# A fused transformer block on one core: 46 instead of 36 expert units beside the selection matrix, in matmuls of 512 columns, five blocks of u in front of the picks, and a parked unit first

## The chip, the cores and the metric

The kernel runs on one core of a Trainium2 chip. The metric is the device time of one execution in microseconds (us), less is better. Engines are named as in the profile: PE does matmuls, ACT is ScalarE, DVE is VectorE, POOL is GpSimd, SP only issues transfers here.

## The reference

Two transformer blocks on 256 tokens of 1024 features in fp32. The change touches only the last layer of the second block, a "PEER" layer: for every token it selects 8 x 16 of 16384 experts, and each expert is a row of u and a row of v.

```python
s = jnp.einsum('thpd,hpnd->thpn', q, sub_keys)
sv, si = lax.top_k(s, k)
...
experts = jnp.take_along_axis(cand_idx, top_i, axis=-1)
g = jax.nn.softmax(top_v, axis=-1)
u_e = u[experts]
v_e = v[experts]
a = jax.nn.gelu(jnp.einsum('td,thkd->thk', xb, u_e).astype(jnp.float32), approximate=False)
return jnp.einsum('thk,thkd->td', (g * a).astype(xb.dtype), v_e)
```

## The kernel before

The kernel gathers nothing. It computes the Gelu of every expert with every token, multiplies by a matrix G (experts by tokens) that holds the softmax weight where the expert was picked and zero elsewhere, and multiplies the product with all of v. Experts are handled in 64 units of 256.

**fp32 as pairs.** Each fp32 operand is split in a rounded part "hi" and a remainder "lo", and a product is three: hi by hi, hi by lo, lo by hi. Weights come in blocks of 512 KB through a ring of five slots: SP issues the load when PE has released the slot, ACT writes hi (L1051), DVE (L1437) or POOL (L2085) writes lo. Beside G all remainders are POOL's. A unit of u is two such blocks (b = 0, 1), a unit of v is two as well.

**Two forms of a block of u.** `feature_panel` (L654, L659) takes the tokens' hi and lo in two matmuls of 256 columns that add up in one PSUM bank per unit. `unit_panel` (L681, L686) streams tokens' hi and lo as one matmul of 512 columns; the products with hi and with lo then lie in two halves of a bank, a unit needs two banks, and somebody must add the halves. Before, only the main part uses the second form: DVE copies one half and adds the other (L2035, L2036).

**Stages.** "Select" finds the picks: DVE works through top-16 lists while PE computes scores and the first 11 units of u. Then the stage "beside G": after two blocks of u, PE transposes the picks (L1008); from there on 64 steps of G (four tokens each) lie between the blocks of u of 36 units. A step of G is: DVE compares (L1984, L1987), ACT scales (L1388), DVE scales the rest (L1994), PE does four matmuls (L1017) in two halves of a bank each, ACT copies one part of the result (L1375), DVE adds the other (L2001), which frees the bank. ACT and DVE do the result of step q - 2 in step q (`HOT_BUFS`). The finished u units go through Gelu (`early_out`, L1345) and are parked in DRAM.

**Main part.** `UNIT_ORDER` mixes the 17 units of u that are left with the 47 parked ones. PE does a unit's u when its turn comes and, `V_LAG` = 2 turns later, its v (L716, L721: 24 matmuls of 512 columns onto four accumulator banks). In between DVE multiplies by G (L2042), ACT rounds (L1406), DVE takes the remainder (L1738).

**The order** is written out by generators that every engine walks: `expert_matrix_order` yields u blocks, the picks and G steps, and a constant (`GELU_LATER`) says how many items later ACT does the Gelu. Each engine takes its own list in order and waits on semaphores. Banks come from `take(..., among=...)`: the first idle one of a group, in the order in which they became idle.

Of the kernel before, what the change touches and what calls it, by code (L numbers as in the profile page):

```python
# [30 lines left out]
T = 256  # L31
# [22 lines left out]
for _name, _n in (("norm_mix_g", 8), ("q_norm_g", 3), ("kv_norm_g", 2), ("b_gate", 16), ("norm_ffn_g", 8),  # L54
# [17 lines left out]
HID_BUFS = 3  # L72
# [4 lines left out]
EARLY_BESIDE_G = 36  # L77
# [20 lines left out]
    early=(22528, 23040, 23552, 52288),  # L98
# [186 lines left out]
def build(nc, a, out, parked_x, parked_g2, parked_units):  # L285
    from contextlib import ExitStack
    ctx = ExitStack()
    with ctx:
# [71 lines left out]
        def psum(*key):  # L360
            return banks[use_of[key][0]]
# [66 lines left out]
        early_stored = [sem(f"early{i}_stored") for i in range(4)]  # L428
# [155 lines left out]
        def tensor_program(e):  # L584
# [451 lines left out]
        def scalar_program(e):  # L1036
# [385 lines left out]
        def vector_program(e):  # L1422
# [580 lines left out]
            for what, n, b in expert_matrix_order():  # L2003
                if what == "u":
                    lo_until(("uT", n), b, 1)
                elif what == "picks":
                    for t in range(NT):
# [8 lines left out]
                else:  # L2016
# [4 lines left out]
            for q in range(N_G - HOT_BUFS, N_G):  # L2021
                G_sum(q)
# [217 lines left out]
        def sync_program(e):  # L2240
# [56 lines left out]
            sp.wait_ge(g2_parked, 16)  # L2297
            for at in range(N_UNITS + V_LAG):
                if at < N_UNITS and UNIT_ORDER[at] >= EARLY:
                    load_until(("uT", UNIT_ORDER[at]))  # L2300
                if at >= V_LAG:
                    v = at - V_LAG
                    load_until(("v", v))
                if at + 1 < N_UNITS and UNIT_ORDER[at + 1] < EARLY:
                    i, u = (at + 1) % HID_BUFS, UNIT_ORDER[at + 1]
                    sp.wait_ge(*(hid_used["peer", at + 1 - HID_BUFS] if at + 1 >= HID_BUFS else full("G", N_G - 1, TG - TG_BANK)))
                    b, nth = early_slot(u)
                    sp.wait_ge(early_stored[b], 16 * (nth + 1))
                    e.dma_start(hid_raw[i], parked_units[u].rearrange("p (c t) -> p c t", t=T)).then_inc(hid_in[i], 16)
# [84 lines left out]
```

## Time and profile before

| | us |
|---|---|
| median of 3 runs | 1392.35 (1391.27 to 1392.82) |
| the profiled execution: its own time | 1391.79 |
| its span in the profile | 1390.0 |
| PE busy | 1351.1 |
| DVE busy | 1017.1 |
| ACT busy | 756.5 |
| POOL busy | 460.1 |

The span runs from the first to the last instruction; the execution's own time is 1.8 us more. Times in rows are microseconds from the start of the span. A row of the order of time merges instructions of one kind; its second number is the time from the start of the first to the end of the last, and since matmuls overlap in the array, the next row starts before that end. "[x <-E name]" is idle time of the engine in front of the row and what ended it. "PEclk" is the granted clock of PE as a share of full speed.

### The profile page before, as it was taken

To read this page: it belongs to the slowest core of one execution; us is meant where nothing else is said; L and a number is where in the kernel's file an instruction comes from. 1 tells how busy PE (TensorE), PEld (TensorE's weight loads), DVE (VectorE), ACT (ScalarE), POOL (GpSimd) and SP (SyncE) were. 2 spreads that over 40 slices of the span, in tenths; PEclk is the share of its full clock that TensorE was granted. 3 is DMA by queue.
4 is the path that set the end of the run, shared out by engine and by line. 5 is a ranking of instruction groups with operands and counts; after the bars stand their busy time and mean duration, and the time that the engine had idled before them with its cause. 6 is when DMAs were issued, how large, how long until landed. Compare 5 with 4: busy or idle time off the path is not lost.

```text
span 1390.0 us, 21698 instructions
## 1 busy us (share of the span) xinstructions
PE 1351.1 (97%) x8475; PEld 1214.4 (87%) x8475; DVE 1017.1 (73%) x1834; ACT 756.5 (54%) x1201; POOL 460.1 (33%) x264
## 2 busy tenths in 40 slices
PE   9999999999999999999799999989999999999997
PEld 7898889999988777999799999987888888888885
DVE  5676686888867675799888888865666666667666
ACT  5555745444656454554477777754444544544543
POOL 2630000000034102798867777641222222222221
PEclk9999999999999999999999999999999999999999
DMA  7553247879878624467566666654757756767665
GB/s 250 179 146 103 78 172 244 277 266 326 274 245 284 242 99 167 137 207 226 175 185 199 200 191 195 207 184 166 232 200 227 235 197 232 234 198 229 231 200 211
DMA packets 194645, 286.69 MB, mean 206 GB/s; under 512 B 9664, under 2 KB 121024, under 8 KB 194288
## 3 DMA queue, kind: packets, MB, share of 16 engines
q1 hardware_dynamic: 186800, 270.12, 60.2%
q10 hardware_dynamic: 7344, 13.95, 2.6%
q0 software_dynamic: 400, 1.25, 0.4%
q8 instruction: 67, 1.10, 0.3%
q14 instruction: 34, 0.28, 0.1%
HBM read 270.34 MB, written 14.94 MB: 205 GB/s over the span
## 4 chain that ended last, share of the span: by engine, by line
PE 81%; DVE 11%; ACT 2%; DMA 2%; POOL 1%; issue 1%; DVEq 0%; ACTq 0%
PE bank L716 19%; PE bank L654 19%; PE bank L721 10%; PE bank L659 9%; PE bank L627 6%; PE bank L681 5%; PE bank L631 3%; PE bank L686 2%; PE bank L1017 2%; DMA sb_raw<-w_in 1%; PE bank L931 1%; PE bank L950 1%; DVE sb_in_row L1930 1%; PE bank L809 1%; DVE sb_eq L1936 1%
## 5 line engine op out<-in xcount | busy, mean ns | idle before, releaser
L2085 POOL TENSOR_TENSOR sb_lo<-sb_raw,sb_hi 128x1024 fp32r<-128x1024 f32 (+1 forms) x162 | 387.7, 2402 | 596.4 <-ACT sb_hi L1051 596.4
L1051 ACT ACTIVATE sb_hi<-sb_raw 128x1024 fp32r<-128x1024 f32 (+2 forms) x428 | 442.3, 1046 | 202.5 <-DMA sb_raw<-w_in 43.0
L1437 DVE TENSOR_TENSOR sb_lo<-sb_raw,sb_hi 128x1024 fp32r<-128x1024 f32 (+2 forms) x266 | 357.0, 1357 | 159.8 <-ACT sb_hi L1051 158.5
L654 PE MATMUL bank<-sb_act,sb_hi 128*128 128x256 f32 x2720 | 357.4, 284 | 0.7 <-DVE sb_act L1523 0.7
L654 PEld LDWEIGHTS bank<-sb_act,sb_hi 128*128 128x128 f32 x2720 | 340.3, 192 | 2.3 <-issue 1.3
L716 PE MATMUL bank<-sb_hi,sb_hid_hi 128*128 128x512 f32 x600 | 234.8, 391 | 4.1 <-DVE sb_hid_lo L1738 4.1
L716 PE MATMUL bank<-sb_hi,sb_hid_lo 128*128 128x512 f32 x600 | 234.5, 391 | 0.0
L659 PE MATMUL bank<-sb_act,sb_lo 128*128 128x256 f32 x1360 | 191.2, 283 | 2.3 <-POOL sb_lo L2085 2.3
L659 PEld LDWEIGHTS bank<-sb_act,sb_lo 128*128 128x128 f32 x1360 | 175.3, 192 | 3.1 <-POOL sb_lo L2085 3.1
L721 PE MATMUL bank<-sb_lo,sb_hid_hi 128*128 128x512 f32 x600 | 161.0, 389 | 0.0
L716 PEld LDWEIGHTS bank<-sb_hi,sb_hid_hi 128*128 128x128 f32 x600 | 113.3, 189 | 27.1 <-DVE sb_hid_lo L1738 4.3
L716 PEld LDWEIGHTS bank<-sb_hi,sb_hid_lo 128*128 128x128 f32 x600 | 113.3, 189 | 22.9
L721 PEld LDWEIGHTS bank<-sb_lo,sb_hid_hi 128*128 128x128 f32 x600 | 112.6, 188 | 23.4
L1406 ACT ACTIVATE sb_hid_hi<-sb_hid 128x512 fp32r<-128x512 f32 x64 | 40.5, 632 | 127.5 <-DVE sb_hid L2042 127.5
L2091 POOL TENSOR_TENSOR sb_stat<-sb_stat 128x1 f32<-128x1 f32 (+1 forms) x19 | 12.6, 673 | 281.8 <-DVE sb_stat L1467 234.1
L1984 DVE TENSOR_TENSOR sb_hot<-bank,sb_pick_T 128x1024 fp32r<-128x1024 f32 x64 | 78.4, 1224 | 31.8 <-PE bank L1017 31.8
L1738 DVE TENSOR_TENSOR sb_hid_lo<-sb_hid,sb_hid_hi 128x512 fp32r<-128x512 f32 x75 | 51.9, 693 | 52.4 <-ACT sb_hid_hi L1406 44.7
L627 PE MATMUL bank<-sb_hi,sb_act 128*128 128x512 f32 (+1 forms) x352 | 83.9, 380 | 1.0 <-DVE sb_act L1523 0.6
L1453 DVE CUSTOM_DVE_ANT_0 sb_ada_junk<-sb_ada_w,sb_c_rows 128x1024 bf16<-128x1024 f32 x64 | 79.4, 1275 | 0.0
L627 PEld LDWEIGHTS bank<-sb_hi,sb_act 128*128 128x128 f32 x352 | 63.2, 188 | 13.1 <-ACT sb_hi L1051 1.9
L681 PE MATMUL bank<-sb_act,sb_hi 128*128 128x512 f32 x272 | 68.6, 395 | 3.2 <-DVE sb_G L2001 3.2
L681 PEld LDWEIGHTS bank<-sb_act,sb_hi 128*128 128x128 f32 x272 | 50.4, 190 | 13.2 <-issue 3.4
(346 smaller groups left out, 1581.5 us busy)
## 6 DMA issues: line engine op xcount, KB each, us to landing
sb_raw<-peer_uT SPq DMA_DIRECT2D x128, 512.0 KB, 4.0
sb_raw<-peer_v SPq DMA_DIRECT2D x128, 512.0 KB, 4.5
sb_raw<-w_in SPq DMA_DIRECT2D x52, 512.0 KB, 4.5
sb_ada_w<-ada_wT SPq DMA_DIRECT2D x48, 512.0 KB, 6.0
parked_units<-sb_early ACTq DMA_DIRECT2D x47, 256.0 KB, 4.1
sb_hid<-parked_units SPq DMA_DIRECT2D x47, 256.0 KB, 2.7
sb_raw<-w_gate SPq DMA_DIRECT2D x22, 512.0 KB, 4.0
sb_raw<-w_up SPq DMA_DIRECT2D x22, 512.0 KB, 5.1
```

Of the source, the lines that this page charges most:

```text
L627: e.matmul(opened[t][:, 0:n], part[:, k0 + k, t * P:(t + 1) * P], hi[:, k, :], start=i == first_i and k == 0 and part is x.hi, stop=False)
L654: e.matmul(bank[:, j * T:(j + 1) * T], hi[:, k, j * P:(j + 1) * P], part[:, k0 + k, :], start=i == first_i and j == 0 and k == 0 and part ...
L659: ins = e.matmul(bank[:, j * T:(j + 1) * T], lo[:, k, j * P:(j + 1) * P], x.hi[:, k0 + k, :], start=False, stop=i == last_i and j == 1 and ...
L681: e.matmul(bank[j][:, :].rearrange("p (w t) -> p w t", w=2), hi[:, k, j * P:(j + 1) * P], act_both[:, k0 + k], start=first and k == 0, sto ...
L716: e.matmul(psum(acc, 2 * half_ + t)[:, :], part[:, k, t * P:(t + 1) * P], hi[:, k, :], start=first and k == 0 and part is hid.hi, stop=False)
L721: ins = e.matmul(psum(acc, 2 * half_ + t)[:, :], hid.hi[:, k, t * P:(t + 1) * P], lo[:, k, :], start=False, stop=last and k == 1)
L1051: e.activation(flat_of(i, "hi"), flat_of(i, "raw"), ACT.Copy).then_inc(hi_done[i % R], 1)
L1437: e.tensor_tensor(flat_of(i, "lo"), flat_of(i, "raw"), flat_of(i, "hi").bitcast(F32), ALU.subtract).then_inc(lo_done[i % R], 1)
L1453: e.tensor_tensor_reduce(ada_junk[n % 2], ada_bufs[b], c_rows[:, row], 1.0, 0.0, ALU.mult, ALU.add, mcol[name][:, c:c + 1]).then_inc(*ada_ ...
L1738: e.tensor_tensor(hid_pair[i].lo, hid_raw[i], hid_pair[i].hi.bitcast(F32), ALU.subtract).then_inc(*hid_lo.inc(*unit))
L1984: e.tensor_tensor(h[:, :, 0:3:2, :].rearrange("p t w n -> p w t n"), iota_p.unsqueeze(1).unsqueeze(1).to_broadcast([P, 2, TG, P]), pT[:, 0 ...
L2085: e.tensor_tensor(flat_of(i, "lo"), flat_of(i, "raw"), flat_of(i, "hi").bitcast(F32), ALU.subtract).then_inc(lo_done[i % R], 1)
```

## The change

1. `EARLY_BESIDE_G` goes from 36 to 46: 57 units are parked, 7 are left for the main part.
2. The 46 units use `unit_panel` with two banks each out of four; G has three banks instead of four.
3. Beside G a unit's halves are joined in three steps: ACT copies one half of each bank to SBUF (`early_halves`, 5 items after the block), DVE adds the other and frees the banks (`early_sum`, 6 items), ACT does the Gelu in place and parks it (`early_gelu`, 7 items). A fifth buffer is added, two alternate.
4. Five blocks of u stand in front of the picks instead of two; the first G step comes behind the ninth block instead of the fifth.
5. In the main part the first turn is a parked unit; the last G step's sums are issued behind the last splits, and the accumulator banks are taken only at the first v.

```diff
-EARLY_BESIDE_G = 36
+EARLY_BESIDE_G = 46
-    early=(22528, 23040, 23552, 52288),
+    early=(22528, 23040, 23552, 52288, 50304),
-GELU_LATER = 4
+COPY_LATER, SUM_LATER, GELU_LATER = 5, 6, 7
-G_FROM = 4
+PICKS_FROM, G_FROM = 5, 8
-UNIT_ORDER = [v for k in range(N_LATE) for v in (EARLY + k, *range(k * EARLY // N_LATE, (k + 1) * EARLY // N_LATE))]
+UNIT_ORDER = [0] + [v for k in range(N_LATE) for v in (EARLY + k, *range(1 + k * (EARLY - 1) // N_LATE, 1 + (k + 1) * (EARLY - 1) // N_LATE))]
...
-    return 3, u - EARLY_BESIDE_SELECT
+    return 3 + (u - EARLY_BESIDE_SELECT) % 2, (u - EARLY_BESIDE_SELECT) // 2
...
-        if b == G_FROM // 2 - 1:
+        if b == PICKS_FROM - 1:
             yield "picks", 0, 0
...
-            u_banks, G_banks = idle_banks[0:3], idle_banks[3:7]
+            u_banks, G_banks = idle_banks[0:4], idle_banks[4:7]
...
-                        early_panel = feature_panel(("uT", n), act_T, h2, u_banks)
+                        early_panel = unit_panel(n, h2, u_banks)
...
-            for b in range(4):
-                take("peer_acc", b)
...
+                    if v == 0:
+                        for b in range(4):
+                            take("peer_acc", b)
...
+            def early_halves(u):
+                b, nth = early_slot(u)
+                act.wait_ge(early_stored[b], 16 * nth)
+                for j in range(2):
+                    act.wait_ge(*full(("uT", u), j))
+                    e.activation(early_buf[b][:, j * T:(j + 1) * T], psum(("uT", u), j)[:, T:2 * T], ACT.Copy).then_inc(*early_left.inc(u, j))
+            def early_gelu(u):
+                b, nth = early_slot(u)
+                for j in range(2):
+                    act.wait_ge(*freed(("uT", u), j))
+                e.activation(early_buf[b], early_buf[b], ACT.Gelu).then_inc(*act_self.inc())
+                act.wait_ge(*act_self.at())
+                e.dma_start(parked_units[u], early_buf[b]).then_inc(early_stored[b], 16)
...
-                if at >= GELU_LATER:
-                    what, n, b = order[at - GELU_LATER]
-                    if what == "u" and b == 1:
-                        early_out(n)
-            for q in range(N_G - HOT_BUFS, N_G):
-                G_rounded(q)
+                if at == len(order):
+                    G_rounded(N_G - 2)
+                for later, do in ((COPY_LATER, early_halves), (GELU_LATER, early_gelu)):
+                    if 0 <= at - later < len(order):
+                        what, n, b = order[at - later]
+                        if what == "u" and b == 1:
+                            do(n)
+            hi_until(("uT", UNIT_ORDER[1]), None, 0)
+            G_rounded(N_G - 1)
...
+            def early_sum(u):
+                for j in range(2):
+                    v = early_buf[early_slot(u)[0]][:, j * T:(j + 1) * T]
+                    dve.wait_ge(*early_left.at(u, j))
+                    e.tensor_tensor(v, psum(("uT", u), j)[:, 0:T], v, ALU.add).then_inc(*gives(("uT", u), j))
...
                 elif what == "picks":
+                    early_sum(EARLY_BESIDE_SELECT)
...
+            load_hid(0)
```

**PE, two G steps with the block between them, with their waits.** `bankN_free` is the semaphore of a PSUM bank, `hot_done` DVE's last operation of the step. Before:

```order
1568 L1017 MATMUL bank<-sb_hot_168 128x256 [waits hot_done,bank2_free]
1570 L1017 MATMUL bank<-sb_hot_168 128x256 [waits bank7_free]
...
1572 L654 MATMUL bank<-sb_act,sb_hi_52 128x256 [waits hi0_done]
1574 L659 MATMUL bank<-sb_act,sb_lo_51 128x256 [waits lo0_done]
1576 L1017 MATMUL bank<-sb_hot_169 128x256 [waits hot_done,bank0_free]
1578 L1017 MATMUL bank<-sb_hot_169 128x256 [waits bank6_free]
```

Of the change:

```order
1604 L1018 MATMUL bank<-sb_hot_169 128x256 [waits hot_done,bank2_free]
1606 L1018 MATMUL bank<-sb_hot_169 128x256 [waits bank7_free]
...
1608 L682 MATMUL bank<-sb_act,sb_hi_60 128x512 [waits hi2_done,bank0_free,bank5_free]
1610 L687 MATMUL bank<-sb_act,sb_lo_59 128x256 [waits lo2_done]
1612 L1018 MATMUL bank<-sb_hot_170 128x256 [waits hot_done,bank6_free]
1614 L1018 MATMUL bank<-sb_hot_170 128x256 [waits bank2_free]
```

Before, two steps in a row use four different banks (2, 7, 0, 6). Now the second half of a step waits for bank 2, which the first half of the step before it filled, and a new unit of u waits for two banks.

**ACT beside G, a stretch of the repeating list.** `sb_early` are the buffers of parked units, `sb_G` the result of a G step, `sb_hot` its scaled rows. Before:

```order
505 L1375 ACTIVATE sb_G<-bank 128x128x2 x2
506 L1388 ACTIVATE sb_hot_169<-sb_hot_169,sb_w_hi 128x128 x2
507 L1051 ACTIVATE sb_hi_56<-sb_raw_54 128x1024
508 L1375 ACTIVATE sb_G<-bank 128x128x2 x2
509 L1388 ACTIVATE sb_hot_168<-sb_hot_168,sb_w_hi 128x128 x2
510 L1051 ACTIVATE sb_hi_60<-sb_raw_58 128x1024
511 L1345 ACTIVATE sb_early_166<-bank 128x512
512 L1347 DMA parked_units<-sb_early_166 128x512
```

Of the change, where two blocks without a G between them are one unit:

```order
515 L1377 ACTIVATE sb_G<-bank 128x128x2 x2
516 L1406 ACTIVATE sb_hot_169<-sb_hot_169,sb_w_hi 128x128 x2
517 L1385 ACTIVATE sb_early_166<-bank 128x256 x2
518 L1053 ACTIVATE sb_hi_52<-sb_raw_50 128x1024
519 L1053 ACTIVATE sb_hi_56<-sb_raw_54 128x1024
520 L1391 ACTIVATE sb_early_166<-sb_early_166 128x512
521 L1393 DMA parked_units<-sb_early_166 128x512
522 L1377 ACTIVATE sb_G<-bank 128x128x2 x2
```

And where they belong to two units:

```order
769 L1406 ACTIVATE sb_hot_169<-sb_hot_169,sb_w_hi 128x128 x2
770 L1053 ACTIVATE sb_hi_64<-sb_raw_62 128x1024
771 L1391 ACTIVATE sb_early_167<-sb_early_167 128x512
772 L1393 DMA parked_units<-sb_early_167 128x512
773 L1053 ACTIVATE sb_hi_68<-sb_raw_66 128x1024
774 L1385 ACTIVATE sb_early_166<-bank 128x256 x2
775 L1377 ACTIVATE sb_G<-bank 128x128x2 x2
```

Before, at most a split and a Gelu lie between the scaled rows of one step and the G copy of the next. Now two splits or one, two copies and a Gelu with its transfer lie there.

**ACT at the start of the main part, of the change.** `sb_hid` is a unit on its way to v, the first split is the second block of unit 57, the three later ones belong to v.

```order
1065 L1391 ACTIVATE sb_early_167<-sb_early_167 128x512 [waits bank0_free,bank5_free]
...
1067 L1053 ACTIVATE sb_hi_56<-sb_raw_54 128x1024 [waits slot1_in]
1068 L1377 ACTIVATE sb_G<-bank 128x128x2 [waits bank7_full]
...
1070 L1427 ACTIVATE sb_hid_hi_126<-sb_hid_123 128x512 [waits hid_gated]
1071 L1053 ACTIVATE sb_hi_60<-sb_raw_58 128x1024 [waits slot2_in]
```

Before, four splits were done in this place in front of the first product. Now one stands in front of the last G copy, and those of v come behind the first rounded unit.

## Rows read from the trace of the kernel before

**Rows 1.** The page, part 1: busy time, share of the span, instructions.
```profile
PE 1351.1 (97%) x8475; PEld 1214.4 (87%) x8475; DVE 1017.1 (73%) x1834; ACT 756.5 (54%) x1201; POOL 460.1 (33%) x264
```

**Rows 2.** Stages: window, us, busy of PE, PEld, DVE, ACT, POOL; PEclk, DMA, GB/s.
```profile
680.00:700.00 20.00, 13.06 (x97) 12.89 (x97) 17.67 (x23) 8.29 (x13) 13.66 (x6) 0.83 0.41 132
740.00:780.00 40.00, 40.00 (x336) 40.00 (x335) 33.02 (x56) 30.19 (x63) 29.02 (x13) 1.00 0.66 198
```

**Rows 3.** In order of time, around the picks: PE, DVE, ACT, POOL.
```profile
691.59 0.66 PE L1008 MATMUL bank<-sb_const,sb_pick 128*128 128x128 f32 x2 [6.94 <-DVE sb_weight L1972]
692.75 3.10 PE L654 MATMUL bank<-sb_act,sb_hi 128*128 128x256 f32 x16
...
689.20 2.24 DVE L1972 TENSOR_TENSOR sb_weight<-sb_topv,sb_stat 128x256 f32<-128x256 f32 x1
...
687.67 2.95 ACT L1051 ACTIVATE sb_hi<-sb_raw 128x1024 fp32r<-128x1024 f32 x3 [0.40 <-ACT sb_early L1345]
...
688.80 7.20 POOL L2085 TENSOR_TENSOR sb_lo<-sb_raw,sb_hi 128x1024 fp32r<-128x1024 f32 x3 [4.62 <-ACT sb_hi L1051]
```

**Rows 4.** In order of time, PE beside G: one block and one G.
```profile
876.16 2.08 PE L654 MATMUL bank<-sb_act,sb_hi 128*128 128x256 f32 x16
...
878.08 1.12 PE L659 MATMUL bank<-sb_act,sb_lo 128*128 128x256 f32 x8
...
879.04 0.64 PE L1017 MATMUL bank<-sb_hot 128*128 128x256 f32 x4
...
879.52 2.08 PE L654 MATMUL bank<-sb_act,sb_hi 128*128 128x256 f32 x16
```

**Rows 5.** The same stretch, DVE and ACT; last, the group of G copies.
```profile
876.36 1.23 DVE L1984 TENSOR_TENSOR sb_hot<-bank,sb_pick_T 128x1024 fp32r<-128x1024 f32 x1 [0.38 <-PE bank L1017]
877.62 0.70 ACT L1388 ACTIVATE sb_hot<-sb_hot,sb_w_hi 128x128 fp32r<-128x128 f32 x2 [0.82 <-DVE sb_hot L1984]
...
877.96 0.80 DVE L2001 TENSOR_TENSOR sb_G<-bank,sb_G 128x256 f32<-128x256 f32 x2
...
878.23 1.05 ACT L1051 ACTIVATE sb_hi<-sb_raw 128x1024 fp32r<-128x1024 f32 x1
878.67 0.68 DVE L1994 TENSOR_TENSOR sb_hot<-sb_hot,bank 128x512 fp32r<-128x512 f32 x1
...
879.30 0.60 ACT L1345 ACTIVATE sb_early<-bank 128x512 f32<-128x512 f32 x1
...
880.30 0.69 ACT L1375 ACTIVATE sb_G<-bank 128x256 f32<-128x256 f32 x2 [0.40 <-ACT sb_early L1345]
...
L1375 ACT ACTIVATE sb_G<-bank 128x256 f32<-128x256 f32 x128 | 44.3, 405 | 19.1 <-ACT sb_early L1345 11.7 <-PE bank L1017 7.4
```

**Rows 6.** Transfers, 720 to 900 us: count, KB each, median us to landing.
```profile
sb_raw<-peer_uT SPq DMA_DIRECT2D x54, 512.0 KB, 4.0
```

**Rows 7.** In order of time, PE in the main part: two blocks of u, v.
```profile
948.01 1.98 PE L681 MATMUL bank<-sb_act,sb_hi 128*128 128x512 f32 x8
949.82 1.12 PE L686 MATMUL bank<-sb_act,sb_lo 128*128 128x256 f32 x8
...
953.57 0.40 PE L716 MATMUL bank<-sb_hi,sb_hid_hi 128*128 128x512 f32 x1
...
959.04 0.39 PE L716 MATMUL bank<-sb_hi,sb_hid_hi 128*128 128x512 f32 x1
```

**Rows 8.** In order of time, PE from the stage beside G to the main part.
```profile
925.12 1.12 PE L659 MATMUL bank<-sb_act,sb_lo 128*128 128x256 f32 x8
929.48 2.94 PE L681 MATMUL bank<-sb_act,sb_hi 128*128 128x512 f32 x8 [3.24 <-DVE sb_G L2001]
...
940.98 0.80 PE L716 MATMUL bank<-sb_hi,sb_hid_hi 128*128 128x512 f32 x1 [4.12 <-DVE sb_hid_lo L1738]
...
944.34 1.08 PE L721 MATMUL bank<-sb_lo,sb_hid_hi 128*128 128x512 f32 x4
```

More of the change, by code:

```diff
@@ L427, in build @@
         ctx_in, mid_g_in = sem("ctx_in"), sem("mid_g_in")
-        early_stored = [sem(f"early{i}_stored") for i in range(4)]
+        early_stored = [sem(f"early{i}_stored") for i in range(5)]
+        early_left = Events(sem("early_left"), [(u, j) for u in range(EARLY_BESIDE_SELECT, EARLY) for j in range(2)])
         hid_in = [sem(f"hid{i}_in") for i in range(HID_BUFS)]
@@ L667, in feature_panel, with unit_panel @@
                 give(key)
-            def unit_panel(u, ready):
+            def unit_panel(u, ready, among=range(8)):
                 key = ("uT", u)
-                bank = [take(key, j) for j in range(2)]
+                bank = [take(key, j, among=among) for j in range(2)]
                 k0 = 0
@@ L2001, in G_sum @@
                     e.tensor_tensor(v, psum("G", q, j0)[:, :].rearrange("p (t w i) -> p w i t", t=TG_BANK, w=2)[:, 1], v, ALU.add).then_inc(*gives("G", q, j0))
-            for what, n, b in expert_matrix_order():
+            def early_sum(u):
[3 more added lines that the diff above has]
+                    e.tensor_tensor(v, psum(("uT", u), j)[:, 0:T], v, ALU.add).then_inc(*gives(("uT", u), j))
+            order = list(expert_matrix_order())
+            for at in range(len(order) + SUM_LATER):
+                what, n, b = order[at] if at < len(order) else ("", 0, 0)
                 if what == "u":
@@ L2015, in vector_program @@
                     own(e.tensor_copy(w_hi_row, w_hi.bitcast(F32).rearrange("p (q j) -> p q j", j=TG)[:, :, TG_ACT:TG]))
-                else:
+                elif what == "G":
                     hot_equal(n)
@@ L2020, in vector_program @@
                     hot_left(n)
-            for q in range(N_G - HOT_BUFS, N_G):
-                G_sum(q)
+                if at == len(order):
+                    G_sum(N_G - 2)
+                if at >= SUM_LATER:
+                    what, n, b = order[at - SUM_LATER]
+                    if what == "u" and b == 1 and n > EARLY_BESIDE_SELECT:
+                        early_sum(n)
+            lo_until(("uT", UNIT_ORDER[1]), None, 0)
+            G_sum(N_G - 1)
             e.tensor_copy(best[:, 0:1], iota_p[:, 0:1]).then_inc(*gives("numbers"))
@@ L2297, in sync_program, with load_hid @@
             sp.wait_ge(g2_parked, 16)
+            def load_hid(at):
+                i, u = at % HID_BUFS, UNIT_ORDER[at]
+                sp.wait_ge(*(hid_used["peer", at - HID_BUFS] if at >= HID_BUFS else full("G", N_G - (1 if at else 2), TG - TG_BANK)))
+                b, nth = early_slot(u)
+                sp.wait_ge(early_stored[b], 16 * (nth + 1))
+                e.dma_start(hid_raw[i], parked_units[u].rearrange("p (c t) -> p c t", t=T)).then_inc(hid_in[i], 16)
+            load_hid(0)
             for at in range(N_UNITS + V_LAG):
@@ L2304, in sync_program @@
                 if at + 1 < N_UNITS and UNIT_ORDER[at + 1] < EARLY:
[L2305 to L2309, printed above, removed]
+                    load_hid(at + 1)
             load_until(("end_g",))
```

## The prediction

> **What bounds the kernel now.** I read the page's busy shares first: PE is busy 1351.1 of 1390.0 us [rows 1]. The stage table then says where this is tight: between 740 and 780 us PE is busy 40.00 of 40.00, with ACT at 30.19, DVE at 33.02 and POOL at 29.02, at a granted clock of 1.00; between 680 and 700 PE is busy only 13.06 of 20 [rows 2]. So the change can win in three ways only: fewer PE nanoseconds per block of u, less PE idle time before the picks, and less at the seam between the stage beside G and the main part. It can lose where an engine that is busy 75 to 80% gets more to do in front of something that PE waits for.
>
> **The form of a block.** Before, a block beside G is 24 matmuls of 256 columns: from 876.16 to 879.04, 16 in 1.92 and 8 in 0.96: 2.88 us, 120 ns each [rows 4]. The main part already runs the other form: 8 matmuls of 512 columns from 948.01 to 949.82, 1.81 us, 226 ns each, and two whole blocks from 948.01 to 953.57, so 2.78 a block [rows 7]. The 72 blocks of the 36 units gain 0.10 each, **7.2 us**. The 20 blocks of the other 10 units move from the main part at 2.78 to the same 2.78: nothing. G (four matmuls, 0.48) and v (953.57 to 959.04, 5.47 a unit) keep their prices [rows 4, 7]. In the Trainium skill, the page "TensorE: Matmul & The Clock Gate", section "Back-to-back issue gap", gives an isolated gap of N/2.4 + 2.5 ns, so 109 ns for 256 columns and 216 for 512, by which one wide matmul costs what two narrow ones do and the 72 blocks would gain 1.2 us. The rows say 120 and 226, and I go by them.
>
> **In front of the picks.** PE idles 6.94 us for the weights, and its next 16 matmuls take 2.94 (692.75 to 695.69) where 1.92 is usual, with 0.16 lost in the transposes: 8.1 us in all [rows 3]. Now three more blocks stand there. The first has its split ready and runs to 687.1 (PE's idle time began at 691.59 - 6.94 = 684.65, less 0.16 of a matmul's end, and a block is 2.78). The next waits for ACT, which is held by the exponential until 687.67 and then splits (0.98 each), and for POOL, 688.80 plus 2.4 [rows 3]: PE idles 1.7, then 0.6 for the remainder. The fifth block needs the two banks of the first unit. DVE frees them only after the weights (689.20 + 2.24 = 691.44 [rows 3]) and ACT only after four splits (about 691.6) and two copies: about 693.1, another 0.9. Behind the picks the banks of the next units come late twice, as long as no G lies between the blocks: a copy stands behind a split whose slot was freed 4.2 us earlier (transfer 4.0 [rows 6] and the issue), about 0.75 each, and 0.35 once at G3. Sum 5.25 against 8.1: **2.85 us gained**.
>
> **The seam.** Before: PE ends u at 926.08 (925.12 + 0.96), starts the first v matmul at 940.98, and its first eight take 3.36 (to 944.34) where 1.8 is usual. For 5.56 us of blocks that is 9.3 + 1.5 = 10.9 us lost, 3.24 and 4.12 of it idle [rows 8]; the first wide matmuls ran partly at the lower clock (2.94 instead of 1.98 for eight, to the end of the last [rows 7, 8]). After: unit 0 is parked, so its v needs only the last G sum, the product, rounding and remainder. From the end of u (zero): ACT copies and Gelu of the last unit until 2.2, the split of the second block of unit 57 until 3.2, G rounded 3.85, DVE sum 4.4. POOL makes that block's remainder until 5.65; PE loses 0.5 and 0.6. DVE's product, two SBUF operands beside a POOL operation, I let wait for it: 6.3, rounded and remainder 7.6, the split of v behind them 8.0: 1.4 lost. Unit 57's own chain (three remainders of v on DVE, copies, sums, Gelu, product) ends 2.7 after PE is done with the first v. Sum 5.2, no clock fall assumed: **5.7 less 0.5 for half a chance of one, 5.2 us gained**.
>
> **What the form costs the others.** Per unit ACT gets two copies from PSUM and a Gelu from SBUF (about 0.55 + 1.0 with its DMA) for one Gelu (1.0), DVE two sums (0.72). Per four blocks and three G that leaves ACT some 10.8 of 12.6 us and DVE 10.3: on average both fit. But ACT takes its queue in order, and the G banks fell from four to three: the second half of each G now takes the bank of the first half of the G before (the order rows in the part on the change), where before it had a whole G longer. That bank needs ACT's rounding and DVE's sum. Set zero where PE starts the block behind a G, 876.16 [rows 4, 5]: DVE starts its comparison at 0.20, could start its sum 1.60 later, ends at about 3.1; ACT starts its scaled rows at 1.46 and is free for a split at 2.07; a split takes 1.05, Gelu with its DMA 1.0 (879.30 to 880.30), one G copy 0.40. PE wants the second half of the next G but one at 2.78 + 0.48 + 2.78 + 0.24 = 6.28. Doubles (two blocks with no G between) come every four blocks and lie in two ways:
>
> Where the double is one unit (u16 u17), ACT has behind the second G after it: copies (2.62), split (3.6), a split whose slot PE left just before zero, so data at 3.75, done 4.83, Gelu and DMA to 5.85, and only then the G copy, 6.25. DVE's sum ends 6.7, PE starts at 6.80: **0.52 late**. Eight such places: 4.2 us.
>
> Where it straddles two units (u75 u76), Gelu must wait for DVE's sums (3.92), then Gelu 4.95, split 6.0, copies 6.55, G copy 6.95, sum 7.4, PE 7.50: **1.22 late**. Seven places: 8.5 us.
>
> Three runs of five blocks give 0.7, 0.7 and 1.1: 2.5 us. Together **15.2 us lost**. After each double PE does 5.56 us of u, in which ACT and DVE catch up, so lateness does not pile up. The bounds: nothing if the G copy gets through before the split (ACT then has 2 us to spare), 34 us if each of the 18 places loses one operation more (a split, 1.05).
>
> **Main part.** Eight parked units now stand in a row, 1.25 MB for 5.47 us of v. Splits of v wait for DMA briefly today without PE waiting; I cost it at nothing. The cover is two blocks of v ahead; without it each v could lose up to 0.5.
>
> **Sum** against the profiled run's own 1391.79: -7.2 - 2.85 - 5.2 + 15.2 = -0.05, so 1391.7; that run lies 0.6 below the median of the others, well inside what I can tell. 0.2% is 2.8 us, about what a measurement of this kernel can tell from no change.
>
> **The rivals.**
> (1) *ACT is not late* (28%). Average load speaks for it, 86%, and in the first pattern it is a wait for DMA that puts ACT behind; if slots come 0.5 earlier, or the first sum comes in before the split, most of the 15.2 goes, and 7.2 + 2.85 + 5.2 stays: 1376.5, up to 1383 with 40% of the stalls. Against it: each of the times above is a row, and the order of ACT's queue is fixed.
> (2) *ACT falls behind for good* (10%), the other side: in the straddling pattern ACT ends a round about 0.8 us before it must start the next, with PE's round then 13.8 us. From some 8% on top of its operations' durations (0.8 of 10.8) lateness goes over to the next round; at 11% each of the 22 rounds loses 0.4 more: 1400.5.
> (3) *The transfers of eight parked units in a row hold v up* (7%): 0.1 to 0.2 us each of 56 units, 1397 to 1402. For it: more bytes per us than any stretch of v has now. Against: PE never waits for DMA in the main part.
> (4) *Wide matmuls gain little beside G* (3%): 1.2 instead of 7.2, 1397.7. The rule named above would give it; the rows of the same form in the main part speak against.
> (5) *Seam and picks gain nothing* (2%): 1399.
>
> **The numbers.** The worked case holds 50%, own range 1386 to 1397 (stalls 12 to 20, seam and picks each 2 either way): faster 15, same 22, slower 13 of 100. Rival 1 adds 28 to faster, 2 to 5 add 22 to slower. Faster 0.43, same 0.22, slower 0.35. The range takes the top of rival 1 and the bottom of 2 and 3: 1377 to 1399.
>
> **What would show it.** Wide form: L682 eight in 1.8 us and 2.78 a block beside G. Stalls: PE idle before L1018 with DVE sb_G L2022 as releaser, 18 times or so, 0.5 and 1.2 us, and before that DVE waiting for ACT's sb_G; if these rows are absent, rival 1. Picks: idle before the picks under 3 us instead of 6.94, and no slow matmuls behind. Seam: first v within 9 us of the last u. If PE has idle rows in the middle of the main part, rival 3. Wrong altogether if ACT in the stage shows no place where its G copy follows a split and a Gelu.

## The result, and the profile after

| | before | after |
|---|---|---|
| time, median of 20 runs each (us) | 1391.60 (1390.51 to 1394.12) | 1394.56 (1392.59 to 1398.48) |
| ratio after/before | | 1.0019, 95% interval 1.0012 to 1.0025 |
| profiled execution, own time / span (us) | 1391.79 / 1390.0 | 1393.27 / 1391.4 |

The change makes the kernel 3.0 us slower by the medians. The interval of the ratio does not include 1, so my forecast of no change (1391.7) was wrong, by a small amount. Of the 3.0 the two profiled executions show 1.5. The rest is scatter that the profiled one does not have: half of the executions of after lie 1.3 or more above it.

The page of after, part 1, answers to [rows 1]:

```profile
PE 1348.7 (97%) x7899; PEld 1181.8 (85%) x7899; DVE 1013.1 (73%) x1871; ACT 774.2 (56%) x1293; POOL 496.5 (36%) x279
```

What PE waited for (us in total, times, longest), whole execution:

```profile
PE bank L682 <- DVE sb_early L2028: 6.9, 11, 1.7
PE bank L1018 <- DVE sb_G L2022: 4.4, 12, 1.3
...
PE bank L717 <- DVE sb_hid_lo L1759: 2.2, 1, 2.2
```

The first two kinds of wait do not exist before the change. The windows, with the columns of [rows 2]:

```profile
680.00:700.00 20.00, 17.84 (x101) 15.00 (x100) 15.66 (x22) 9.94 (x15) 15.32 (x7) 1.00 0.57 180
740.00:780.00 40.00, 39.55 (x236) 34.85 (x235) 31.02 (x58) 30.74 (x68) 29.54 (x13) 1.00 0.67 205
780.00:820.00 40.00, 38.15 (x225) 33.27 (x224) 31.86 (x58) 29.53 (x65) 27.95 (x13) 1.00 0.62 192
...
1300.00:1340.00 40.00, 40.00 (x186) 33.41 (x185) 26.66 (x28) 19.24 (x23) 9.61 (x4) 1.00 0.66 219
```

In front of the picks PE is now busy 17.84 of 20 instead of 13.06. Beside G it is no longer at 40.00. In the main part it is.

In order of time around one unit boundary beside G, PE, then DVE, then ACT (start, us, operation, tiles, count, and in brackets the idle time before it and who ended it):

```profile
796.84 1.07 PE L682 MATMUL bank<-sb_act,sb_hi 128*128 128x512 f32 x4
797.75 1.11 PE L687 MATMUL bank<-sb_act,sb_lo 128*128 128x256 f32 x8
798.70 0.64 PE L1018 MATMUL bank<-sb_hot 128*128 128x256 f32 x4
799.86 2.08 PE L682 MATMUL bank<-sb_act,sb_hi 128*128 128x512 f32 x8 [0.52 <-DVE sb_early L2028]
801.77 1.11 PE L687 MATMUL bank<-sb_act,sb_lo 128*128 128x256 f32 x8
802.73 0.40 PE L1018 MATMUL bank<-sb_hot 128*128 128x256 f32 x2
803.36 0.50 PE L1018 MATMUL bank<-sb_hot 128*128 128x256 f32 x2 [0.23 <-DVE sb_G L2022]
803.70 1.99 PE L682 MATMUL bank<-sb_act,sb_hi 128*128 128x512 f32 x8
805.52 1.12 PE L687 MATMUL bank<-sb_act,sb_lo 128*128 128x256 f32 x8
806.47 2.00 PE L682 MATMUL bank<-sb_act,sb_hi 128*128 128x512 f32 x8
...
797.71 0.79 DVE L2022 TENSOR_TENSOR sb_G<-bank,sb_G 128x256 f32<-128x256 f32 x2
798.42 0.67 DVE L2015 TENSOR_TENSOR sb_hot<-sb_hot,bank 128x512 fp32r<-128x512 f32 x1
799.01 0.74 DVE L2028 TENSOR_TENSOR sb_early<-bank,sb_early 128x256 f32<-128x256 f32 x2
799.68 1.21 DVE L2005 TENSOR_TENSOR sb_hot<-bank,sb_pick_T 128x1024 fp32r<-128x1024 f32 x1
...
802.82 0.83 DVE L2022 TENSOR_TENSOR sb_G<-bank,sb_G 128x256 f32<-128x256 f32 x2 [1.47 <-ACT sb_G L1377]
...
799.85 0.63 ACT L1391 ACTIVATE sb_early<-sb_early 128x512 f32<-128x512 f32 x1 [0.84 <-DVE sb_early L2028]
...
800.89 1.06 ACT L1053 ACTIVATE sb_hi<-sb_raw 128x1024 fp32r<-128x1024 f32 x1 [0.40 <-ACT sb_early L1391]
801.85 0.64 ACT L1385 ACTIVATE sb_early<-bank 128x256 f32<-128x256 f32 x2
802.38 0.77 ACT L1377 ACTIVATE sb_G<-bank 128x256 f32<-128x256 f32 x2
```

Three things are to be read here. (a) *The unit wait.* G ends at 799.18 (798.70 + four times 0.12), and the next unit starts at 799.86, 0.68 later (the 0.52 of the row counts from the last matmul's end in the array, 0.16 later): its banks are freed by DVE's sum, issued at 799.01 behind a G sum and DVE's scaling of the rest of the rows. (b) *The G wait.* The second half of the next G starts 0.39 late (802.73 + 0.24, against 803.36). DVE's G sum (802.82) waited 1.47 for ACT's G copy (802.38), which stands behind a Gelu that waited 0.84, a split and two copies. (c) *The slow restart.* After the wait eight wide matmuls take 1.91 (799.86 to 801.77), after no wait 1.85 (806.47 to 808.32, the start of the next row in the same view) and 1.82 (803.70 to 805.52). Two G matmuls after a wait take 0.34 (803.36 to 803.70) instead of 0.24.

I count 29 places beside G from 713 us on where PE starts late: 10 unit waits of 0.67 to 0.69 (6.75 us) and 19 G waits of 0.20 to 1.45 (8.15 us), 14.9 together. Between the G at 733.53 and the one at 982.63 lie 249.1 us, 74 blocks and 56 G: 74 x 2.79 + 56 x 0.48 is 233.3, so 15.8 are lost. The 26 late starts in that stretch are 13.3 of it. The other 2.5 are almost all slow restarts: the rows behind the late starts show 0.10 for each of 18 G waits and 0.06 to 0.09 for each of 8 unit waits, **2.3 us**. Over the whole stage they are 2.5.

The seam of after, PE in order of time, answers to [rows 8]:

```profile
1002.53 1.07 PE L722 MATMUL bank<-sb_lo,sb_hid_hi 128*128 128x512 f32 x4
1005.77 0.50 PE L717 MATMUL bank<-sb_hi,sb_hid_hi 128*128 128x512 f32 x1 [2.18 <-DVE sb_hid_lo L1759]
1006.11 0.39 PE L717 MATMUL bank<-sb_hi,sb_hid_lo 128*128 128x512 f32 x1
1006.34 0.39 PE L717 MATMUL bank<-sb_hi,sb_hid_hi 128*128 128x512 f32 x1
```

The long waits of [rows 8] are gone; one of 1.03 stays in front of the first v (997.92), and one of 2.18 at the second.

### The profile page after: what moved, and what is told of

Read it like the earlier page. It is cut to its first block, busy times and chain, and to the rows that moved or that the text cites. A ratio compares the mean times of both kernels' runs of the same rounds, so it can differ in the third digit from the quotient of the medians.

```text
span 1391.4 us, 20757 instructions
## 1 busy us (share of the span) xinstructions
PE 1348.7 (97%) x7899; PEld 1181.8 (85%) x7899; DVE 1013.1 (73%) x1871; ACT 774.2 (56%) x1293; POOL 496.5 (36%) x279
## 3 DMA queue, kind: packets, MB, share of 16 engines
q8 instruction: 63, 1.03, 0.3%
## 4 chain that ended last, share of the span: by engine, by line
PE 69%; DVE 16%; ACT 6%; issue 3%; DMA 3%; POOL 1%; ACTq 1%; DVEq 0%
PE bank L717 19%; PE bank L722 9%; PE bank L655 9%; PE bank L682 8%; PE bank L628 6%; PE bank L660 5%; PE bank L687 4%; PE bank L632 3%; ACT sb_hi L1053 2%; DVE sb_hot L2005 2%; PE bank L1018 1%; DMA sb_raw<-peer_uT 1%; DVE sb_lo L1458 1%; DVE sb_G L2022 1%; PE bank L932 1%
## 5 line engine op out<-in xcount | busy, mean ns | idle before, releaser
L2121 POOL TENSOR_TENSOR sb_lo<-sb_raw,sb_hi 128x1024 fp32r<-128x1024 f32 (+1 forms) x177 | 423.1, 2406 | 562.7 <-ACT sb_hi L1053 562.7
L1458 DVE TENSOR_TENSOR sb_lo<-sb_raw,sb_hi 128x1024 fp32r<-128x1024 f32 (+2 forms) x251 | 335.3, 1355 | 143.0 <-ACT sb_hi L1053 142.0
L682 PE MATMUL bank<-sb_act,sb_hi 128*128 128x512 f32 x848 | 213.3, 393 | 9.0 <-DVE sb_early L2028 6.9
L655 PE MATMUL bank<-sb_act,sb_hi 128*128 128x256 f32 x1568 | 206.1, 284 | 1.0 <-DVE sb_act L1544 0.7
L655 PEld LDWEIGHTS bank<-sb_act,sb_hi 128*128 128x128 f32 x1568 | 195.5, 192 | 2.5 <-issue 1.1
L682 PEld LDWEIGHTS bank<-sb_act,sb_hi 128*128 128x128 f32 x848 | 152.5, 188 | 39.2 <-DVE sb_early L2028 9.2
L687 PEld LDWEIGHTS bank<-sb_act,sb_lo 128*128 128x128 f32 x848 | 115.5, 190 | 9.7 <-POOL sb_lo L2121 1.6
L687 PE MATMUL bank<-sb_act,sb_lo 128*128 128x256 f32 x848 | 118.4, 282 | 0.7 <-POOL sb_lo L2121 0.7
L660 PE MATMUL bank<-sb_act,sb_lo 128*128 128x256 f32 x784 | 110.4, 283 | 2.4 <-POOL sb_lo L2121 2.3
L660 PEld LDWEIGHTS bank<-sb_act,sb_lo 128*128 128x128 f32 x784 | 101.1, 192 | 3.2 <-POOL sb_lo L2121 3.2
```

Of the source, the lines that this page charges most:

```text
L655: e.matmul(bank[:, j * T:(j + 1) * T], hi[:, k, j * P:(j + 1) * P], part[:, k0 + k, :], start=i == first_i and j == 0 and k == 0 and part ...
L660: ins = e.matmul(bank[:, j * T:(j + 1) * T], lo[:, k, j * P:(j + 1) * P], x.hi[:, k0 + k, :], start=False, stop=i == last_i and j == 1 and ...
L682: e.matmul(bank[j][:, :].rearrange("p (w t) -> p w t", w=2), hi[:, k, j * P:(j + 1) * P], act_both[:, k0 + k], start=first and k == 0, sto ...
L687: ins = e.matmul(bank[j][:, 0:T], lo[:, k, j * P:(j + 1) * P], act_T.hi[:, k0 + k, :], start=False, stop=last and k == kb - 1, skip_group_ ...
L1458: e.tensor_tensor(flat_of(i, "lo"), flat_of(i, "raw"), flat_of(i, "hi").bitcast(F32), ALU.subtract).then_inc(lo_done[i % R], 1)
L2121: e.tensor_tensor(flat_of(i, "lo"), flat_of(i, "raw"), flat_of(i, "hi").bitcast(F32), ALU.subtract).then_inc(lo_done[i % R], 1)
```

## The experiments

Before measured 1391.55 to 1391.98 in all of them. The "narrow" kernels take back the 512-column form beside G and leave the rest of the change. Medians, and ratios to before with 95% intervals:

| run | what differs | us | ratio |
|---|---|---|---|
| e4_same | the change, unaltered | 1394.35 | 1.0018 (1.0009 to 1.0027) |
| e1_narrow | narrow form, 4 banks for G | 1381.70 | 0.9928 (0.9915 to 0.9942) |
| e8_three | narrow, 3 banks for G | 1381.75 | 0.9927 (0.9913 to 0.9940) |
| f_picks | narrow, 2 blocks before the picks, first G behind the fifth | 1389.14 | 0.9981 (0.9971 to 0.9991) |
| f_unit | narrow, no parked unit in front | 1385.25 | 0.9952 (0.9939 to 0.9965) |
| e7_two | narrow, two parked units in front | 1382.45 | 0.9929 (0.9916 to 0.9942) |
| e10_v_first | the same, split of v first | 1380.27 | 0.9916 (0.9903 to 0.9929) |
| e3_no_gelu | the change without Gelu beside G | 1385.35 | 0.9961 (0.9948 to 0.9975) |
| e5_gelu9 | copies, sums, Gelu at 5, 6, 9 | 1391.19 | 0.9994 (0.9984 to 1.0003) |
| e2_later | 5, 5, 9 | 1397.82 | 1.0044 (1.0030 to 1.0057) |
| e6_458 | 4, 5, 8 | 1384.28 | 0.9943 (0.9928 to 0.9958) |
| e11_best | 4, 5, 8, two parked, split of v first | 1383.07 | 0.9937 (0.9925 to 0.9949) |

**e4_same.** 

> The changed kernel once more, for its scatter: its 20 runs lay between 1392.6 and 1398.5, those of before between 1390.5 and 1394.1. Theory: the waits beside G hang on when ACT's DMA waits end, so a slower execution shows more or longer idle rows in front of L1018 and L682, and nothing else differs. Rival: a slower execution loses its time elsewhere (clock, main part). Median 1394.5.

Same time as after, as expected. Its profile is worth more than its time, since it fell on one of the longer executions (span 1393.8, 2.4 above that of after). The theory fails: the last G stands at 986.54 us in it and at 986.64 in after, so the stage beside G costs both the same. The rival holds, and it has two parts. The first is the clock. Window 1005 to 1010 us, after and then e4_same:

```profile
1005.00:1010.00 5.00, 4.22 (x19) 3.49 (x20) 3.07 (x4) 2.53 (x3) 1.98 (x1) 1.00 0.77 256
```

```profile
1005.00:1010.00 5.00, 4.33 (x12) 3.46 (x13) 3.10 (x4) 2.52 (x3) 2.09 (x1) 0.67 0.73 253
```

Behind the wait at the second v (2.12 here, 2.18 there) the granted clock is 1.00 in one and 0.67 in the other, in PE's rows of e4_same:

```profile
1005.67 0.50 PE L717 MATMUL bank<-sb_hi,sb_hid_hi 128*128 128x512 f32 x1 [2.12 <-DVE sb_hid_lo L1759]
...
1006.72 0.63 PE L717 MATMUL bank<-sb_hi,sb_hid_hi 128*128 128x512 f32 x1
1007.14 0.63 PE L717 MATMUL bank<-sb_hi,sb_hid_lo 128*128 128x512 f32 x1
```

0.42 from start to start is the 1.2 GHz level, where 0.227 is usual. From 1005.67 to 1010.11 it takes 4.44 for 12 matmuls that take 2.86 in after (1005.77 to 1008.63): 1.6 us. By the last matmul 1.3 of it is left (1383.40 against 1382.11). The second part, the other 1.05, lies behind that: DVE's first sum of the end waits for a transfer, in after and then in e4_same, and in every profile the end of the span comes 12.35 to 12.38 behind the start of this sum.

```profile
1379.07 0.70 DVE L2091 TENSOR_TENSOR bank<-bank,sb_slot 128x512 f32<-128x512 f32 x1 [3.85 <-DMA sb_slot<-parked_g]
```

```profile
1381.41 0.70 DVE L2091 TENSOR_TENSOR bank<-bank,sb_slot 128x512 f32<-128x512 f32 x1 [4.86 <-DMA sb_slot<-parked_g]
```

From the issue of this transfer to the sum pass 4.70 us in after, 5.74 in e4_same and 5.49 in before.

Nine of the profiles (after, e4_same and seven of the runs below) have the same wait of 2.12 to 2.18 us at the second v. In five of them matmuls at 0.42 follow (e4_same, e2_later, e6_458, e8_three, f_picks), in four none does (after, e1_narrow, e3_no_gelu, e5_gelu9). Each of the five loses some 1.6 us by them.

**e1_narrow.**

```diff
-COPY_LATER, SUM_LATER, GELU_LATER = 5, 6, 7
+GELU_LATER = 4
-            u_banks, G_banks = idle_banks[0:4], idle_banks[4:7]
+            u_banks, G_banks = idle_banks[0:3], idle_banks[3:7]
-                        early_panel = unit_panel(n, h2, u_banks)
+                        early_panel = feature_panel(("uT", n), act_T, h2, u_banks)
```

Copies and `early_sum` go with it, and the Gelu is again taken from the bank.

> The changed kernel (46 units, five blocks in front of the picks, first G behind the ninth block, unit 0 first in the main part) with the form of a block beside G undone: 24 matmuls of 256 columns, one bank a unit out of three, four banks for G, one Gelu from PSUM four items later. Theory: the waits for banks beside G cost some 17 us, the wide form gives back 6.5, and picks and seam gained 2.5 and 6. Then the stage has no idle rows in its middle, the 20 moved blocks cost 0.09 more each, and the time is 1391.6 - 2.5 - 6 + 1.8 = 1385, 1383 to 1388. Rival (the other edits gave nothing, or more units beside G cost by themselves): 1391 or more.

1381.70, 3.3 below my number and below the range that I gave. Beside G, PE has no wait (740 to 980 us: 240.00 busy of 240). The 3.3 come from the picks and the seam, where I had left part of the lateness: with u's banks free earlier, PE loses 2.1 from the first block of the stage to the first G instead of 5.2, and 4.1 at the seam instead of 4.9. So the form costs **12.9 us** in place of a gain. The profiled executions account for it: 92 blocks at 0.087 less (-8.0), stalls +14.9, restarts +2.5, picks +3.1, seam +0.8, less 0.35 by which after enters the stage earlier and 0.4 that e1_narrow loses at 1099 us: 12.5 against a difference of spans of 12.6.

**e8_three** (as e1_narrow, with `idle_banks[4:7]` for G).

> The narrow form as in the 46-unit narrow run (1381.7), but G has three banks instead of four, as in the change; nothing else. If three banks for G need ACT's extra work of the wide form to become a stall (theory), a few G waits of 0.1 to 0.4 appear at most: 1382.5 (1381 to 1384.5). If the missing fourth bank alone makes the stalls (rival), PE waits at L1018 in some 18 places by 0.5: 1390 or more.

1381.75, no G wait at all. The missing fourth bank alone costs nothing; the G waits need ACT's longer queue as well.

**e3_no_gelu** leaves out the Gelu of the 46 units beside G, so these are parked without it.

```diff
-                e.activation(early_buf[b], early_buf[b], ACT.Gelu).then_inc(*act_self.inc())
-                act.wait_ge(*act_self.at())
```

> The changed kernel without the Gelu of the 46 units beside G, whose values go out unrounded by it (so part of the computation is missing); copies, sums and transfers stay. ACT is 0.66 us a unit shorter in front of the late G copies. Theory: the waits in front of G matmuls (about 0.4 us, some 25 places) go, those of a new unit's first block for DVE's sum (0.68, nine places) stay: 1394.6 - 9 = 1385.5, 1383 to 1389. If waits were DVE's doing: unchanged within 2 us.

1385.35, as expected. What PE waited for:

```profile
PE bank L682 <- DVE sb_early L2026: 6.7, 12, 0.9
PE bank L810 <- DVE sb_prob_T L1553: 2.8, 6, 0.8
```

The G waits are gone without a rest, and the unit waits stand as before. So there are two mechanisms, and ACT's queue is behind one only.

**e2_later** (`COPY_LATER, SUM_LATER, GELU_LATER = 5, 5, 9`).

> The changed kernel with the Gelu nine items behind the block instead of seven, and DVE's sum five instead of six; nothing else. Theory (the order of ACT's list makes the G copy late, and DVE's sum comes one item late for the next unit's banks): both kinds of waits mostly go, 17 us down to 5 or less, 1394.6 - 12 = 1382.5, 1379 to 1387. Rival (ACT and DVE are loaded too much whatever the order): lateness only moves, 1391 to 1397.

1397.82, wrong by 15 us, and above the rival's range too. The unit waits are gone, but the G waits are 15.6 us in all. DVE and ACT of e2_later, in order of time:

```profile
800.96 0.68 DVE L2015 TENSOR_TENSOR sb_hot<-sb_hot,bank 128x512 fp32r<-128x512 f32 x1
803.66 0.76 DVE L2028 TENSOR_TENSOR sb_early<-bank,sb_early 128x256 f32<-128x256 f32 x2 [2.02 <-ACT sb_early L1385]
...
802.30 1.06 ACT L1053 ACTIVATE sb_hi<-sb_raw 128x1024 fp32r<-128x1024 f32 x1 [0.73 <-DMA sb_raw<-peer_uT]
803.26 0.64 ACT L1385 ACTIVATE sb_early<-bank 128x256 f32<-128x256 f32 x2
```

Copy and sum now stand at the same item: DVE's sum waits 2.02 for a copy that stands behind a split, and that split waits for its transfer. All that DVE does next, the G sums too, is late by it. I had moved the sum and not asked who feeds it.

**e5_gelu9** (5, 6, 9) and **e6_458** (4, 5, 8) take the two moves apart.

> Only the Gelu of a unit beside G comes two items later (GELU_LATER 7 to 9), copies and sums stay at 5 and 6. If ACT's queue behind the second block of a unit is what makes DVE's G sum late, the G waits of PE at L1018 (about 0.3 each) mostly go, while the waits of PE for DVE's early sum (0.68 at the first block of a unit, nine or ten of them) stay: about 3 to 4 us less idle beside G and about 1 us less of slow restarts, 1389.5 (1388 to 1392). If ACT's queue is late whatever stands last in it (rival), the G waits only move: 1394.5 (1393 to 1397).

1391.19, 3.4 below after, inside the range. The G waits of 0.39 behind the unit waits are gone. The eight in front of a whole unit, 0.20 to 0.35 in after, are 0.18 to 0.21 now and did not go: ACT still has one split and the Gelu ahead of the G copy. The ten unit waits stay. New is one G wait of 2.19 at 723 us, where ACT's copies had waited 2.33 for the transfer that frees their buffer, and two have grown to 0.7 to 0.8.

> Copies, sums and Gelu at 4, 5 and 8 items behind their block, in place of 5, 6 and 7: the copies and sums one item earlier, the Gelu one later. If the 0.68 waits at the first block of a unit come only from early_sum standing one item too late in DVE's order, they go, and with the Gelu out of the way few G waits stay: 1384 (1381 to 1388), within 6 us of the narrow form's run. If DVE then waits for ACT's copies behind a split that waits for its transfer, as it did with 5, 5 and 9 (rival), the G waits become 1.2 to 1.7 each: 1394 or more.

1384.28, as the theory said. Its waits of PE:

```profile
PE bank L1018 <- DVE sb_G L2022: 5.4, 13, 1.5
```

and no line for sb_early: the copy and sum one item earlier, with an item between them, remove all ten unit waits, 6.75 us and their restarts, and G waits of 0.33 to 0.59 stay at ten places beside the three near the picks (1.64, 0.89 and 0.69). That shifts by one item each are worth 10 us, and in e2_later minus 3, is the surest reading of the study.

**f_picks** (`PICKS_FROM, G_FROM = 2, 4`) and **f_unit** (`UNIT_ORDER` as before, no `load_hid(0)`), both on the narrow kernel, size the two gains.

> The narrow 46-unit kernel (1381.7) with two blocks before the picks and G from the fourth block again, as before the change (PICKS_FROM, G_FROM = 2, 4). If the five blocks in front of the picks are worth what the two profiles show (8.1 us lost before, 1.95 in the narrow 46-unit kernel), it is 6.2 slower: 1387.9 (1386.5 to 1389.5). If the blocks only move the wait on (rival: worth the 2.85 that I forecast for the change), 1384.5.

1389.14: three more blocks in front of the picks, with one more behind them, are worth 7.4 us where the banks are free. PE's wait for the weights is 6.91 again. My 6.2 rested on 8.1 us lost in before, which leaves out most of the slow transposes: from the first block of the stage to the first G, f_picks loses 9.65, before 8.7 and e1_narrow 2.1.

> The narrow 46-unit kernel (1381.7) with the order of units of before: no parked unit in front, so the main part begins with unit 56, whose u, Gelu and product stand before the first v. If the parked unit is worth what the profiles show (10.9 us lost at the seam before, 3.9 in the narrow 46-unit kernel), it is 7 slower: 1388.7 (1387 to 1390). If half of it came from the early split and remainder alone, which stay (rival), 1385.

1385.25, the rival's number: 3.6 us, less than I expected from the two profiles (7). The seam of f_unit loses 9.0 (6.75 of it idle), not 10.9: the early split and remainder of the next unit, which stay, give 2. The 4.9 left against e1_narrow's seam is reduced by 0.8 that e1_narrow loses before the stage and 0.4 at 1099 us, both outside the part that differs.

**e7_two** and **e10_v_first**: narrow, `UNIT_ORDER = [0, 1] + ...`, and in e10 also:

```diff
+            hi_until(("v", 0), 0, 0)
             for at in range(N_UNITS + V_LAG):
...
                     hid_left(("peer", at), i)
+                    if at == 0:
+                        lo_until(("v", 0), 0, 0)
```

> The narrow form (256-column matmuls beside G, three banks for u, four for G, Gelu straight from the bank) with 46 units and five blocks before the picks, and two parked units first in the main part instead of one. If the idle time of 2.2 to 2.3 us in front of the second v is the chain of unit 57's own product, a parked second unit takes it away, and with it the lower clock behind it: 1381.7 - 2.3 - about 1 = 1378.5 (1377 to 1380), and a smaller scatter. If the wait is for the next splits of v or for the remainder on DVE, not for unit 57 (rival), it stays: 1381.7.

1382.45, above my range of 1377 to 1380: nothing gained. The wait at the second v is gone, and one of 3.02 stands in front of the first, because ACT rounds the second unit before it splits v; seven matmuls at 0.42 follow. PE, then ACT of e7_two, in order of time:

```profile
986.99 0.76 PE L717 MATMUL bank<-sb_hi,sb_hid_hi 128*128 128x512 f32 x1 [3.02 <-ACT sb_hi L1053]
987.55 0.63 PE L717 MATMUL bank<-sb_hi,sb_hid_lo 128*128 128x512 f32 x1
...
983.28 0.63 ACT L1427 ACTIVATE sb_hid_hi<-sb_hid 128x512 fp32r<-128x512 f32 x1 [2.40 <-DVE sb_hid L2073]
985.27 0.63 ACT L1427 ACTIVATE sb_hid_hi<-sb_hid 128x512 fp32r<-128x512 f32 x1 [1.36 <-DVE sb_hid L2073]
985.80 2.94 ACT L1053 ACTIVATE sb_hi<-sb_raw 128x1024 fp32r<-128x1024 f32 x3
```

> Narrow, two parked units in front, and the first split of v (and its remainder) put in front of the second parked unit's work on ACT and DVE. In the kernel with two parked units alone the 2.2 us wait moved from the second v to the first: ACT's split of v (985.80) stood behind the rounding of the second unit, which waits for DVE. If that order is the whole wait, PE starts v at the first unit's remainder, about 984.8 instead of 986.99, and the eight matmuls at 0.43 us instead of 0.23 go too (1.4 us): 1382.4 - 2.2 - 1.4 = 1379 (1378 to 1380.5). If DVE's chain (product, rounding, remainder, two operands each) then holds the second half back (rival), no more than 1 us comes: 1381.5.

1380.27, 2.2 below e7_two and 1.4 below e1_narrow, 1.3 above what I expected. PE's waits of e10_v_first at the seam:

```profile
985.33 0.47 PE L717 MATMUL bank<-sb_hi,sb_hid_hi 128*128 128x512 f32 x1 [0.93 <-DVE sb_hid_lo L1760]
...
988.48 0.50 PE L717 MATMUL bank<-sb_hi,sb_hid_hi 128*128 128x512 f32 x1 [0.16 <-ACT sb_hi L1053]
...
995.52 0.50 PE L717 MATMUL bank<-sb_hi,sb_hid_hi 128*128 128x512 f32 x1 [1.28 <-ACT sb_hi L1053]
```

So the order of ACT's list made the wait of 3.02, but a new one of 1.28 stands at the third v. None of these is long, and the clock is 1.00 behind each. In the two profiles the late starts of the seam are 3.5 us in e7_two and 3.7 here, and the slow matmuls 1.5 and 0.5: the gain that they show is in the slow matmuls. They show 0.8 of the 2.2; the profile here fell on the slowest of its five executions, and the rest is open. It is the fastest kernel of the study, 0.84% below before.

**e11_best** (4, 5, 8 with both of these).

> The 512-column form with copies, sums and Gelu at 4, 5 and 8 (1384.3), two parked units in front and the split of v first. If the two parts add up (the seam 3 to 4 us, from 6.2 us lost there now), 1380.7 (1379.5 to 1382.5), so no better than the narrow form with the same seam (1379), because the waits for G's banks, 7 us in all with their slow restarts and those near the picks, are worth the form's gain. If the wide form still wins by its 9.2 us (rival), 1376.

1383.07, 2.4 above what I expected and outside the range: I had put 3 to 4 us on the seam, and it brings 1.2 against e6_458, as it brings 1.4 in the narrow form. It is 2.8 above e10_v_first: the 512-column form does not win beside G even with the better order. It still loses 3.1 us to three waits for G's banks behind the picks (1.70, 0.73, 0.68), and 4.2 in eleven late starts of 0.17 to 0.47 after that, each with its restart.

## Why the prediction was wrong

**The step that failed** is the price of a late start in the term for the stalls, "Together **15.2 us lost**". The late starts themselves are 14.9. But I priced each as idle time alone; every one is followed by a slow restart, 2.5 us over the stage, which stands in the sum at nothing. A second term was mis-sized: the form gains 6.0, not 7.2, since a block beside G takes 2.79 and not 2.78, and the 20 blocks moved there from the main part pay this too. Picks and seam gained 1.5 more than I gave them, the stalls cost 0.3 less, and with 0.3 lost before the stage and 0.8 gained behind the last matmul the profiled execution moved by 1.5 in all.

The other 1.3, by which the median of after lies above its profile, is not settled. The sum has "no clock fall assumed" and takes 0.5 for half a chance of one. The wait at the second v, which I had foreseen (its chain "ends 2.7 after PE is done with the first v"), is followed by the lower clock in five of nine profiles, at some 1.6 us each; the profile of after is one of the four without. If the other executions of after fall as often as the nine, that makes 0.9 of the 1.3. The transfer at the end, 4.70 in after and 5.74 in e4_same, is the other part that varies. How the 20 executions divide between the two no run shows.

**Term by term**, from the two profiled executions:

| term | forecast | measured |
|---|---|---|
| before the stage | 0 | +0.3 |
| form | -7.2 | -6.0 (2.79 a block, not 2.78) |
| picks | -2.85 | -3.5 (8.7 lost before, 5.2 after) |
| seam | -5.2 | -6.1 (4.8 lost) |
| stalls beside G | +15.2 | +14.9 |
| restarts beside G | 0 | +2.5 |
| sum | -0.05 | +2.1 |

PE's last matmul starts 2.2 later than before. What stands behind it is 0.8 shorter, which leaves the 1.4 of the spans: that is the transfer of `parked_g`, 4.70 us in the profile of after and 5.49 in that of before, and so luck of the two executions.

In the term for the picks, my items for the kernel after the change add up to 5.05, not to the 5.25 that I wrote, and 5.2 is measured. The 8.1 for before was too low: the transposes take 1.16 us there (691.59 to 692.75) and 0.57 where no long wait stands before them, and I put only 0.16 of this on the wait.

**The mechanism of the stalls was half right.** The G waits are as described: DVE's sum waits for ACT's G copy behind a split and a Gelu. The eight in front of a whole unit are 0.20 to 0.35, not 0.52. In the seven straddling places I put 1.22 on one wait for G's bank; it is two, 0.68 for the *unit's* banks and 0.39 to 0.42 for G's: 1.08. Three more waits for a unit's banks, 2.0 together, I did not have at all. The order rows that I printed had the new wait for two banks in them ("waits hi2_done,bank0_free,bank5_free"), and I followed only G's bank. e3_no_gelu, where one kind goes and the other stays, and e6_458, where it is the reverse, show that they are separate. That the total came out within 0.3 is luck: the eight places are 2.0 too high and the seven 0.9, the runs of five blocks 0.6 too low, and the 2.0 were missing.

**The rivals.** (1) ACT not late: refuted, though e6_458 shows how near it was, one item of order for each of copies, sums and Gelu. (2) Falls behind for good: refuted; the straddling waits are 0.39, 0.39, 0.39, 0.42 in a row, and do not grow. (3) Transfers of parked units: refuted, behind the second v PE of after has no idle time above 0.1 us, and between 1300 and 1340 us it is busy 40.00 of 40.00. (4) Wide matmuls gain little: refuted by 2.79 against 2.88 a block. In the Trainium skill the rule for an isolated gap ("TensorE: Matmul & The Clock Gate", "Back-to-back issue gap"), by which an estimated 1.2 of the 7.2 us would have come, does not describe this stream, and the rows decide. (5) Seam and picks: refuted, f_picks and f_unit give 7.4 and 3.6 in the narrow form, and the profile of after 3.5 and 6.1.

**What the change is made of** after the experiments: five blocks in front, 46 units and the parked unit bring 9.9 us together (e1_narrow); the 512-column form costs 12.9, all of that and 3.0 more. No run changes the number of units alone.

## What to carry to other kernels

A form that saves an engine nanoseconds by giving two others more instructions must be priced at each bank it waits for, the ones it takes newly as well as those it leaves to others with less slack: list for every waiting instruction all its semaphores, and who stands in front of each release. Price a stall as its idle time plus about 0.1 us for the restart. Waits of 2.12 to 2.18 us cost a stretch at the lower clock, 1.6 us of it, in five of nine profiles here, so such a wait costs its idle time and, on average over the nine, some 0.9 more. When work is written out at fixed distances, move the producer together with the consumer and keep an item between them: 4, 5, 8 was 10 us faster than 5, 6, 7, and 5, 5, 9 was 3 us slower. And when a profile is compared with a median, look at what varies between executions before the difference is given to the change.

## What I had not expected of the hardware

- A wait of 0.2 to 0.7 us on PE makes the next matmuls slower: eight of 512 columns 1.91 instead of 1.82 to 1.85 us, two of 256 columns 0.34 instead of 0.24, at a granted clock of 1.00.
- The same wait of 2.12 to 2.18 us at the same place left the clock at 1.00 in four profiles and brought matmuls at 0.42 us in five (for 3.4 us in e4_same); behind waits of 1.55 and 1.69 us near the picks the profile of after shows none at that level.
- The clock can fall after the wait has ended: in e4_same the first matmuls behind it still start 0.23 to 0.33 apart, and from 1006.72 they are 0.42 apart.
- In all profiles but one, DVE's first sum of the end waits for the transfer of `parked_g`, 4.2 to 5.7 us from its issue, so a scatter of up to 1.5 us can come from behind the main part.
